# Order of VectorE's hand-written steps in a hybrid decoder block: first conv chunk first, top-k steps and conv taps placed by a table, conv layer norm later

## What is computed

```
h = RMSNorm(x);  P = h @ w_in                       # one projection for three mixers
A: u = swish(LayerNorm(dwconv31(ca * sigmoid(cg))))   # conv mixer, 512 channels, 31 causal taps
B: score = sum_h relu(iq . ik) * iw  (index, 4 heads); top-128 keys per query, as a mask
   att = softmax(qn . kn + bias, over the selected keys) @ v      # 8 heads of 64
C: xbc = silu(dwconv4(xbc)); chunked state-space scan over 4 chunks of 128; gate silu(z), RMSNorm
x = x + concat(A, B, C) @ w_out
x = x + (silu(fg) * fa) @ w_down,  f = dwconv3(RMSNorm(x) @ w_up)
```

## Time and profile before

| what | value |
|---|---|
| median of three runs | 768.38 us |
| the profiled execution's own time | 770.06 us |
| its span, first to last instruction | 768.3 us |
| mean granted TensorE clock | 0.982 |
| TensorE matmul busy | 729.4 us, 95% |
| VectorE busy | 476.2 us, 62% |
| ScalarE busy | 331.5 us, 43% |
| GpSimd busy | 98.9 us, 13% |
| moved by DMA | 69.46 MB, mean 90 GB/s |

### The profile page before, as it was taken

The page is one execution under the profiler, slowest core; times in us unless marked ns, Lnnn a source line. Parts: engine busy times, 40 slices in busy tenths (PEclk is TensorE's granted clock), DMA queues, the critical chain, the costliest instruction groups (busy, mean ns, idle before and its releaser), DMA issues.

```text
span 768.3 us, 9446 instructions
## 1 busy us (share of the span) xinstructions
PE 729.4 (95%) x3430; PEld 580.7 (76%) x3430; DVE 476.2 (62%) x731; ACT 331.5 (43%) x498; POOL 98.9 (13%) x79
## 2 busy tenths in 40 slices
PE   3999988799999989999969999999999999999998
PEld 2767876676666668888848888888888888888886
DVE  5357899977999957666673656565656665212222
ACT  6245464678546664722443344434443434110110
POOL 2000576642000003333020000000000000000000
PEclk9999999999999999999988999999999999999999
DMA  8541312311111142032221323333243322333302
GB/s 263 150 153 56 110 55 56 110 56 56 55 55 55 56 165 93 23 106 55 82 55 55 110 72 91 109 109 87 77 109 109 98 72 103 110 109 110 104 6 110
DMA packets 78047, 69.46 MB, mean 90 GB/s; under 512 B 5815, under 2 KB 64535, under 8 KB 78015
## 3 DMA queue, kind: packets, MB, share of 16 engines
q1 hardware_dynamic: 77871, 68.51, 28.9%
q10 hardware_dynamic: 144, 0.52, 0.2%
HBM read 66.91 MB, written 2.12 MB: 90 GB/s over the span
## 4 chain that ended last, share of the span: by engine, by line
PE 71%; DVE 12%; ACT 6%; issue 5%; POOL 4%; DMA 1%; SPq 0%; DVEq 0%; POOLq 0%; ACTq 0%
PE bank L1442 62%; DVE u_acc L565 3%; POOL stats L724 2%; DVE w_lo L575 2%; POOL u_acc L744 2%; PE bank L1448 2%; PE bank L1462 2%; ACT w_hi L813 1%; DVE xbcT L1249 1%; DMA x_in<-in_x 1%; PE bank L1684 1%; PE bank L1658 1%; DVE prob L1228 1%; PE bank L1632 1%; ACT prob L928 1%
## 5 line engine op out<-in xcount | busy, mean ns | idle before, releaser
L1442 PE MATMUL bank<-h_hi,w_hi 128*128 128x512 f32 x480 | 192.1, 400 | 1.8 <-DVE h_lo L1080 1.8
L1442 PE MATMUL bank<-h_lo,w_hi 128*128 128x512 f32 x480 | 188.5, 393 | 0.0
L1442 PE MATMUL bank<-h_hi,w_lo 128*128 128x512 f32 x480 | 188.4, 393 | 0.0
L575 DVE TENSOR_TENSOR w_lo<-w_raw,w_hi 128x2048 fp32r<-128x2048 f32 x34 | 79.8, 2348 | 80.7 <-ACT w_hi L813 80.7
L1442 PEld LDWEIGHTS bank<-h_hi,w_hi 128*128 128x128 f32 x480 | 91.2, 190 | 29.3 <-issue 10.6
L1442 PEld LDWEIGHTS bank<-h_hi,w_lo 128*128 128x128 f32 x480 | 91.0, 190 | 19.7
L1442 PEld LDWEIGHTS bank<-h_lo,w_hi 128*128 128x128 f32 x480 | 91.3, 190 | 18.0
L1403 DVE SCALAR_TENSOR_TENSOR f<-bank,prm,f 128x511 f32<-128x511 f32 x88 | 65.8, 747 | 58.1 <-ACT f L1049 51.8
L813 ACT ACTIVATE w_hi<-w_raw 128x2048 fp32r<-128x2048 f32 x34 | 64.9, 1910 | 80.9 <-PE bank L1442 80.3
L1049 ACT ACTIVATE f<-bank,prm 128x512 f32<-128x512 f32 x44 | 33.8, 769 | 102.2 <-PE bank L1442 102.2
L1442 PE MATMUL bank<-w_hi,g_hi 128*128 128x512 f32 x176 | 68.5, 389 | 0.0
(11 more groups left out here) (225 smaller groups left out, 1022.7 us busy)
## 6 DMA issues: line engine op xcount, KB each, us to landing
w_raw<-in_w_up SPq DMA_DIRECT2D x44, 512.0 KB, 4.7
w_raw<-in_w_in SPq DMA_DIRECT2D x34, 512.0 KB, 4.7
w_raw<-in_w_down SPq DMA_DIRECT2D x22, 512.0 KB, 4.4
w_raw<-in_w_out SPq DMA_DIRECT2D x12, 512.0 KB, 4.2
x_in<-in_x SPq DMA_DIRECT2D x4, 512.0 KB, 6.7
tbias<-distance_table SPq DMA_DIRECT2D x1, 2048.0 KB, 8.2
x<-in_x SPq DMA_DIRECT2D x4, 512.0 KB, 6.5
out_x<-y_out SPq DMA_DIRECT2D x8, 256.0 KB, 2.0
```

Source lines behind the costliest of these rows:

```text
L575: eng.tensor_tensor(wlo[:, slot, cols], wraw[:, slot, cols], whi[:, slot, cols].bitcast(F32), ALU.subtract).then_inc(ready, 1)
L1442: ins = pe.matmul(o, a, b, start=first and i == 0 and q == 0, stop=last and i == n - 1 and q == 2)
```

## The change

The chunk of conv 0 comes first and the index chunk second; the index steps of blocks 1 to 3 move to slots 8 to 11, those of block 3 over two slots. The even spreading of the search steps and taps over ranges of slots is replaced by a table, `FILL`, that names for each slot the steps in `fill`, in order: 1, 2, 3 are the next step of the search of that block, a, b, c, d the next tap of conv tile 0, 1, 2, 3. Tile 1 instead of tile 0 is the one that GpSimd adds, in the same slots 15 to 44. The layer norm goes from slots 66 and 67 to 70 and 71, the transposes back from 70 and 71 to 73 and 74, both to the end of the slot (`fill`), and both from the auxiliary ring to the accumulation ring. The x transposes are spread over slots 65 and 66. The number of instructions stays the same.

```diff
-CHUNKS = [("iq", 0), ("conv", 0), ("conv", 1)]
+CHUNKS = [("conv", 0), ("iq", 0), ("conv", 1)]
...
-TOP_SLOTS = {1: (9, 36), 2: (9, 42), 3: (9, 48)}
-DW_SLOTS = [(15, 44), (14, 50), (42, 63), (46, 65)]
-LN_SLOTS = (66, 66, 67, 67)
-LNT_SLOTS = (70, 70, 71, 71)
+FILL = {6: "aa", 7: "aaa", 8: "aaa", 10: "1121", 11: "1212", 12: "31213", 14: "2131", 
+        15: "21321", 16: "32112", 18: "31", 19: "23", 20: "121", 22: "31231", 23: "21a3", 
+        24: "21312a1", 25: "3", 26: "21", 27: "32", 28: "1a2", 30: "31123", 31: "a123", 
+        32: "121a31", 33: "231", 34: "2a13", 35: "213", 36: "2a23", 37: "2", 38: "3a23", 
+        39: "2a323", 40: "2a32", 42: "32a33", 43: "ac3ca", 44: "3c3c", 46: "a3c", 47: "d", 
+        48: "cdacd", 50: "cd", 51: "ac", 52: "dcda", 54: "dcd", 55: "c", 56: "dcadc", 58: "dca", 
+        59: "dc", 60: "dcda", 62: "cddc", 63: "adcd", 64: "cdac", 65: "dc", 66: "dacdc", 
+        67: "ddcd", 68: "cdcdcd", 69: "ccddd"}
+POOL_SLOTS = (15, 44)
+LN_SLOTS = (70, 70, 71, 71)
+LNT_SLOTS = (73, 73, 74, 74)
-DW_POOL = 0
+DW_POOL = 1
...
-    put(3, ("ev", "iq", 0), ("ev", "iq", 1), ("small",), ("ev", "ik", 0))
+    put(3, ("ev", "cg", 0), ("ev", "ca", 0), ("small",), ("ev", "ik", 0))
     put(4, ("iwT",), ("dt", 0))
-    put(6, ("dt", 1))
-    put(8, ("dt", 2))
-    for n, b in ((5, 1), (6, 2), (8, 3)):
-        put(n, *[("idx", b, h) for h in range(NIH)])
-    for b in (1, 2, 3):
-        spread([(k, b, r) for r in range(TOPK // 8) for k in ("topmax", "topmark")], *TOP_SLOTS[b])
-        fill[TOP_SLOTS[b][1]].append(("sel", b))
+    put(5, ("dt", 1))
+    put(6, ("ev", "iq", 0), ("dt", 2))
+    put(8, ("ev", "iq", 1))
+    for n, b, hs in ((8, 1, (0, 1, 2, 3)), (9, 2, (0, 1, 2, 3)), (10, 3, (0, 1)), (11, 3, (2, 3))):
+        put(n, *[("idx", b, h) for h in hs])
...
-        fill[(n if j else at[("conv", 1)]) + 5].append(("glu", j))
-        a, b = DW_SLOTS[j]
-        spread([("dw", j, i) for i in range(CONV_K)], a, b)
+        fill[n + 5].append(("glu", j))
+    spread([("dw", DW_POOL, i) for i in range(CONV_K)], *POOL_SLOTS)
+    spread([("dwp", DW_POOL, i) for i in range(1, CONV_K)], POOL_SLOTS[0] - 1, POOL_SLOTS[1] - 1)
+    for n, letters in FILL.items():
+        fill[n] += [next(streams[v]) for v in letters]
     for t in range(NT):
-        put(LN_SLOTS[t], ("ln", t))
+        fill[LN_SLOTS[t]].append(("ln", t))
         front[LN_SLOTS[t] + 1].append(("lnn", t))
     for j in range(4):
-        put(LNT_SLOTS[j], ("lnT", j))
+        fill[LNT_SLOTS[j]].append(("lnT", j))
...
-    put(s0 + 1, *[("xt", t) for t in range(NT)])
+    for t in range(NT):
+        put(s0 + 1 + t // 2, ("xt", t))
...
-        if k in ("prm", "idx", "ln", "lnT", "qkT", "cs", "iwT", "yT"):
+        if k in ("prm", "idx", "qkT", "cs", "iwT", "yT"):
             aux.append(s)
+        elif k in ("ln", "lnT"):
+            group(*s)
...
-                        ins = pe.matmul(ps("iq", v)[:, :], w[:, kk, v], h[:, kk, :],
+                        ins = pe.matmul(ps("cg" if v == 0 else "ca", 0)[:, :], w[:, kk, v], h[:, kk, :],
...
+                            claim(pe, "cg", 0)
+                            claim(pe, "ca", 0)
                             first_pass(whi, hhi, True, False)
...
                         ins = turn(ps(*s)[:, P * j:P * j + P], u_acc[:, j, P * s[1]:P * s[1] + P])
-                    ins.then_inc(aux_done, 1)
+                    ins.then_inc(acc_step, 1)
```

More of the change, by code:

```diff
@@ L124, in make_plan @@
         fill[4 * c - 3].append(("lo", c))
+    streams = {str(b): iter([(k, b, r) for r in range(TOPK // 8) for k in ("topmax", "topmark")]
+                            + [("sel", b)]) for b in (1, 2, 3)}
+    for j in range(4):
+        streams["abcd"[j]] = iter([("dw", j, i) for i in range(CONV_K)])
     def spread(steps, a, b):
@@ L175, in make_plan @@
         n = at[("conv", j)]
-        put(n + 2, ("ev", "cg", j))
-        put(n + 4, ("ev", "ca", j))
-        fill[(n if j else at[("conv", 1)]) + 5].append(("glu", j))
-        a, b = DW_SLOTS[j]
-        spread([("dw", j, i) for i in range(CONV_K)], a, b)
-        if j == DW_POOL:
-            spread([("dwp", j, i) for i in range(1, CONV_K)], a - 1, b - 1)
+        if j:
+            put(n + 2, ("ev", "cg", j))
+            put(n + 4, ("ev", "ca", j))
+        fill[n + 5].append(("glu", j))
[3 more added lines that the diff above has]
+        fill[n] += [next(streams[v]) for v in letters]
     for t in range(NT):
-        put(LN_SLOTS[t], ("ln", t))
+        fill[LN_SLOTS[t]].append(("ln", t))
         front[LN_SLOTS[t] + 1].append(("lnn", t))
     for j in range(4):
-        put(LNT_SLOTS[j], ("lnT", j))
+        fill[LNT_SLOTS[j]].append(("lnT", j))
     for m in range(8):
```

## The result

The changed kernel takes **779.7 us** (median of four runs, 778.45 to 783.62) against 768.34 (four runs, 765.89 to 770.06): ratio 1.0162, 95% interval 1.0127 to 1.0196. It is 1.6% slower; the forecast was 764.4, with a range up to 773. Its profiled execution took 778.45 us, with a span of 776.7. (It is the fastest of its four, and the profiled execution of before was the slowest of its own; so the traces differ by 8.4 us and the medians by 11.4.)

The account below looks back on a forecast made before the run. TensorE was bound by stops before 403.4 us, mostly for VectorE's badly spread work; the feed-forward part was fixed. Gains of 16 and 4.1 less 16.4 gave 3.7, rounded to 4: 764.4 us in the median, range 752 to 773.

Parts of the forecast that it names:

- The upstream gain: Slots up to 64: spreading VectorE's taps and search steps removes TensorE's stops and lowered clock; 16 us gained, bounds 9 and 19.
- Spread x transposes: Slots 65 and 66: the idle time among the transposes and its lowered clock go; 4.1 us gained, bounds 2.4 and 4.1.
- Conv first: First chunks: loading conv before index changes nothing in the time; zero, bounds minus 1 and plus 1.
- This is where the gain is given back: Later layer norm and last taps behind slot 64: new TensorE waits and lowered clock cost 16.4 us, bounds 5 and 22.
- first y product: Slot 70: TensorE waits 6.5 us because 22 taps stand ahead of the first decay product in VectorE's queue.
- third layer-norm transposes: End of slot 71: they wait about 3.0 us for the bank of slot 70's out-projection group, which VectorE drains late.
- second y product: Slot 74: waits about 3.5 us, as VectorE's second decay product stands behind the layer norm's transposes back.
- slot 76: Conv's out-projection there gets its input in time, within 1 us.
- lowered clock: Behind two of the three late waits TensorE runs at the lower clock level; 3.4 us.
- the third: Rival: VectorE late at slot 64 carries its lateness into slot 70's y product; slower, 774 us; chance 0.13.
- second rival: The GpSimd loop keeps the pace, slot 32 still starting after 131 us; 769 us, no change; chance 0.15.
- the first's: Rival: the layer norm hides, first y product waiting under 2 us; cost 5 or less, time 753 us; chance 0.25.

Follow-up runs that it names:

- the best one: Changed kernel with last 11 taps behind first decay product, second decay product earlier, slot 66's taps in slot 64, drains of slots 70, 72, 74 first: 757.99 us.

## Why the prediction was wrong, point by point

**The upstream gain: right.** 16 us by slot 64 was forecast, 14.8 came; no idle is left before slots 24 and 49, and slot 32 keeps 2.31. The lead grows where the prediction put it: 2.4 to slot 24, 7.1 more to slot 44, 5.3 in slots 44 to 63. (Its list of stops leaves out two of before, 0.43 and 0.35 ahead of slots 30 and 31, which are gone too.) The table `FILL` was never run by itself; that it makes this gain is argued, from VectorE's 57.9 busy us against 57.5 forecast and from the three other parts, which alone gain nothing.

**Spread x transposes: right inside the change, wrong as a part.** 4.1 was counted. From slot 64 to 70 the lead grew by 6.0, of which 1.6 is the norm's forward transposes leaving slots 66 and 67 (0.8 each: slot 67 takes 2.81 us instead of 3.62). But the edit alone gains nothing; it pays only together with the later layer norm. A part that is credited by itself has to be read with the waits that follow it in the same queue.

**Conv first: right**, at zero in the time.

**"This is where the gain is given back": the place was right, the size was not.** The cost was put at 16.4 with an upper bound of 22; it is 29.8. So 3.7 gained became 9.0 lost at slot 77: 13.4 more cost, 1.2 less gain upstream, 1.9 more from slot 64 to 70. (The medians are another 2.4 further apart than that; these two traces don't show why.) Term by term (waits as idle time; a few tenths more in start-to-start):

| term | predicted | measured |
|---|---|---|
| first y product | 6.5 | 8.0 |
| third layer-norm transposes | 3.0 | 2.4 |
| second y product | 3.5 | 3.4 |
| slot 76 | "within 1" | 5.2 |
| lowered clock | 3.4 | about 8 |

These make 27 of the 29.8; 1.6 more is the norm's forward transposes, whose leaving of slots 66 and 67 is in the gain above. Two terms make most of the miss: slot 76 with 5.2 and the clock with 4.5, of which 1.8 is again slot 76's.

- *Slot 76 is the step that failed.* The prediction checked that the layer norm's result is there in time, and it is. It didn't check the bank. It had found for the third transposes, at the end of slot 71, that the out-projection group of slot 70 holds their bank, and used this once. Slot 76 takes the bank of the group of slot 74, whose drain (339.92 in VectorE's rows above) stands behind two conv low parts, the first of which comes after 7.88 us of waiting for ScalarE, and six instructions of the scan's output. The changed kernel has eight groups more in the accumulator ring, which shifts who follows whom: by the kernel's own list of groups, slot 76 took the bank of slot 72 before. Draining first brought 9 us in all; from slot 75 to 77, where only this wait and its clock stand, 9.1 us instead of 15.0.
- *The lowered clock.* Two of three waits at 1.7 each were counted. Three of four did it, and each cost more: from the y product's start to the next slot 6.85 us instead of 3.54 with TensorE kept busy, 7.11 instead of 4.30 in the version that doesn't wait there, and 6.81 instead of 4.99 from slot 76 to 77. That is 3.3 + 2.8 + 1.8 = 7.9. The 1.7 came from stops of 2 to 3 us and was applied to stops of 3.4 to 8.
- *The first wait.* Counted as there, from the end of slot 64 (265.62), TensorE's side was right (21.9 us to the wait, 21.7 forecast). VectorE's was 1.9 longer: the y product starts after 30.1 and not 28.2. Its low part began 6.9 after slot 64, as forecast; what follows took 23.2 and not 21.3. The prediction took 0.68 for each of the 22 taps. Three take 1.44 from start to start, beside GpSimd, 2.3 us more in all; the others were a little faster than 0.68. The row with 1.51 was read, and the prediction priced the effect at zero, since "most taps" show none; it looked at which taps leave GpSimd's side and never at which arrive there. The layer norm was moved past GpSimd's queue too. The Trainium skill ("SBUF — State Buffer", SBUF: two separate sides) describes a port pair that VectorE and GpSimd share, held for a whole instruction. By that rule instructions of the two take turns, and the trace agrees in the main: the three taps start 1.44 us apart and the second and third GpSimd product 1.43. It is somewhat less than one after the other would give, since a tap alone takes 0.64 from start to start and such a product 1.00 (299.68 to 300.68 before), 1.64 together.

**The rivals.** The result lies on the side of the third, but its mechanism isn't it: VectorE was not late at slot 64, it idled there 3.21 us, where the prediction had said 3. The second rival's sign, slot 32 still starting after 131, didn't come (129.25), nor did the first's, a y product that waits under 2 us. The bounds were the weak part: 22 was made of the three named waits at their worst, with no room for a fourth.

**Where the time went.** The table and the late norm are one trade. The late norm lets 22 taps be late, which frees slots 44 to 59; the price is VectorE's order behind slot 64, where four things that TensorE needs stand behind work that is not urgent. Most of the loss isn't the trade's own: with these few moves 12.2 us of a lead of 21 at slot 70 are left at slot 77, and the kernel is faster than before. The remaining waits there are 1.14, 0.64, 2.21 and 1.09.

What stays open: the last idle time at the scan's yb transposes and the remaining 2.31 of slot 32 weren't worked on. Neither the table alone nor the exchange of GpSimd's tile was run by itself.

## What to carry to other kernels

When a step is moved in a hand-written order, go through every engine's queue that it is moved past, and for each later instruction ask two things: is its data there, and is its bank free, which means: who drains the group that had the bank before, and what stands ahead of that drain. Put drains and the products that TensorE waits for ahead of work with slack; here that was worth some 19 us of the 22 between the changed kernel and the best one. Price a wait of TensorE with the clock behind it, by rows with the same kind of matmul.

## What the runs showed of the hardware

- An elementwise GpSimd instruction with two SBUF inputs and a VectorE tap with two SBUF inputs don't run side by side: 1.44 us from start to start instead of 0.64 to 0.68 for each such tap, 1.43 instead of 1.00 for the GpSimd instruction, and one stretched tap fewer as soon as one of the GpSimd products was cut to 64 columns.
- In these slots TensorE came back at the 1.2 GHz level after each idle time of 3.4 us and more, with 3.36 to 3.68 us for sixteen 64-column matmuls against 1.9 to 2.0. Between 1.9 and 2.5 us either happened: the same 1.91 us ahead of the same instruction lowered it in one version (its eight matmuls 1.94 us) and not in another (1.06), 2.48 lowered it in one (1.78) and 2.47 not in another (1.06), and 2.44 among the x transposes lowered it before but not with the first chunks exchanged (slot 66: 5.23 against 3.65). The length alone doesn't tell what a short idle time will cost.
- Keeping TensorE busy with useless matmuls in a wait held the clock here (2.00 us for the sixteen matmuls instead of 3.67). Of the 2.8 us by which slot 71 started earlier, 0.8 was left at slot 77: the next wait grew by 0.9, and behind it the clock fell, as it had not done behind the shorter one. This is one trace against one.
